# Routed expert layer on one core: slot numbers of all blocks fetched once ahead of the loop, gathers queued ahead of scatters, last expert's second weight half loaded later

## What is computed

```python
logits = (xf @ router_w + router_b)
top_vals, top_idx = lax.top_k(logits, TOP_K)      # 4 of 32 experts
gates = jax.nn.softmax(top_vals, axis=-1)
...
def expert_block(args):
    xblk, e = args
    h = xblk @ w1[e] + b1[e]
    g, u = jnp.split(h, 2, axis=-1)
    g = jnp.minimum(g, SWIGLU_LIMIT)
    u = jnp.clip(u, -SWIGLU_LIMIT, SWIGLU_LIMIT)
    act = g * jax.nn.sigmoid(SWIGLU_ALPHA * g) * (u + 1.0)
    return act @ w2[e] + b2[e]
...
y = jnp.zeros((N, D)).at[row_tok].add(yb * row_w[:, None])
```

## Time and profile before

| | |
|---|---|
| median of 3 runs | 2829.48 us (2829.42 to 2830.85) |
| profiled execution, its own time | 2824.4 us |
| its span, first to last instruction | 2822.6 us |
| mean granted TensorE clock | 0.948 |
| PE (matmul) busy | 2552.1 us, 90% of the span |
| DVE / ACT / POOL busy | 744.7 / 362.4 / 499.3 us |
| DMA bytes | 511.69 MB, of them 472.48 MB in SP's queue |

### The profile page before, as it was taken

One profiled execution on the slowest core, in us unless ns is written; L12 is line 12 of the kernel. 1 busy time (PEld: TensorE's weight loads), 2 busy tenths in 40 slices (PEclk: granted clock), 3 DMA queues, 4 the chain that ended last, 5 costly groups with the idle time before them and its releaser, 6 DMA issues.

```text
span 2822.6 us, 59253 instructions
## 1 busy us (share of the span) xinstructions
PE 2552.1 (90%) x22930; PEld 1090.6 (39%) x22931; DVE 744.7 (26%) x2075; ACT 362.4 (13%) x920; POOL 499.3 (18%) x639
## 2 busy tenths in 40 slices
PE   8999899999989769879998997997997999989984
PEld 4644556544435423223332332332332433323322
DVE  4441456411024412112221221221221222212212
ACT  2000455400003200000000000000000000000002
POOL 0000000000001212122221222221222222222221
PEclk9999899999999879889998998998998999999987
DMA  4110000400044495989689767668528357273464
GB/s 141 60 45 0 8 8 1 146 26 23 15 142 146 115 368 208 407 343 341 253 311 406 291 227 294 224 224 310 201 66 332 124 170 274 63 277 121 166 231 142
DMA packets 159463, 511.69 MB, mean 181 GB/s; under 512 B 37540, under 2 KB 73892, under 8 KB 125380
## 3 DMA queue, kind: packets, MB, share of 16 engines
q1 hardware_dynamic: 110576, 472.48, 43.1%
q0 software_dynamic: 29168, 38.39, 7.2%
q10 hardware_dynamic: 19668, 0.15, 0.4%
HBM read 479.16 MB, written 32.15 MB: 181 GB/s over the span
## 4 chain that ended last, share of the span: by engine, by line
PE 39%; DMA 23%; SPq 4%; issue 2%; DVE 1%; ACT 0%; ACTq 0%; POOL 0%; DVEq 0%; POOLq 0%
PE xbank L1487 21%; PE xbank L1510 13%; DMA big<-in_w 10%; DMA idxa<-slot_rows 9%; DMA loop_s<-xn_rows,idxg 4%; PE xbank L1443 4%; SPq L1034 2%; SPq L1039 1%; PE xbank L1497 1%; DMA acc_rows<-loop_s,idxs 0%; PE xbank L1504 0%; DVE big L1404 0%; PE xbank L1428 0%; DVE loop_s L1368 0%; ACT loop_s L1156 0%
## 5 line engine op out<-in xcount | busy, mean ns | idle before, releaser
L1487 PE MATMUL xbank<-big,loop_s 128*32 128x512 f32 x9280 | 1101.6, 612 | 134.0 <-DMA big<-in_w 109.9
L1487 PEld LDWEIGHTS xbank<-big,loop_s 128*32 128x32 f32 x9280 | 282.9, 111 | 788.2 <-issue 602.5
L1510 PE MATMUL xbank<-big,loop_s 128*32 128x256 f32 x9280 | 540.1, 386 | 0.0
L1368 DVE TENSOR_SCALAR loop_s<-xbank 128x256 f32<-128x256 f32 x145 | 61.6, 425 | 1301.3 <-PE xbank L1487 1301.3
L1510 PEld LDWEIGHTS xbank<-big,loop_s 128*32 128x32 f32 x9280 | 288.6, 112 | 247.7 <-issue 63.0
L1150 ACT ACTIVATE loop_s<-loop_s 128x256 f32<-128x256 f32 x145 | 60.5, 417 | 1658.7 <-DVE loop_s L1368 1635.4
L607 PE MATMUL pair<-big 128*128 128x512 f32 (+1 forms) x640 | 253.6, 551 | 0.2 <-DMA big<-in_w_in 0.2
L1086 POOL DMA_INDIRECT acc_rows<-loop_s,idxs x145 | 230.9, 1593 | 123.4 <-POOL idxs L1083 72.5
L1083 POOL TENSOR_TENSOR idxs<-idxa,tok 128x1 int32<-128x1 int32 x145 | 41.7, 288 | 941.9 <-ACT loop_s L1156 796.7
L1076 POOL DMA_INDIRECT loop_s<-xn_rows,idxg x147 | 145.8, 992 | 120.2 <-POOL idxg L1073 112.6
L607 PEld LDWEIGHTS pair<-big 128*128 128x128 f32 x640 | 119.3, 191 | 114.8 <-issue 110.8
(11 more groups left out here) (234 smaller groups left out, 1722.4 us busy)
## 6 DMA issues: line engine op xcount, KB each, us to landing
big<-in_w SPq DMA_DIRECT2D x396, 1024.0 KB, 12.9
big<-in_x SPq DMA_DIRECT2D x16, 512.0 KB, 5.0
big<-in_w_in SPq DMA_DIRECT2D x4, 2048.0 KB, 8.0
big<-in_w_in SPq DMA_DIRECT2D x16, 512.0 KB, 4.0
big<-in_w_o SPq DMA_DIRECT2D x1, 4096.0 KB, 26.9
acc_rows<-big SPq DMA_DIRECT2D x8, 512.0 KB
xn_rows<-big SPq DMA_DIRECT2D x8, 512.0 KB, 4.5
big<-acc_rows SPq DMA_DIRECT2D x8, 512.0 KB, 8.1
```

What stands on the lines that cost most here:

```text
L1368: dve.tensor_scalar(gl, up_bank[b][:, 0:FG], SWIGLU_LIMIT, None, ALU.min).then_inc(gate_min, 1)
L1487: ins = pe.matmul(up_bank[b][QB * c:QB * c + QB, :].rearrange("p (h k q) -> p h k q", h=2, q=QB), xT[b][:, QB * k:QB * k + QB], w1k[b][k]. ...
L1510: ins = pe.matmul(y_bank[b][QB * j:QB * j + QB, 0:DG], actT[b][:, QB * k:QB * k + QB], w2r[b][:, k, j * DG:(j + 1) * DG], start=False, sto ...
```

## The change

Ahead of the loop, POOL now issues two indirect DMAs that fetch the table rows of all blocks (one table row of 32 slots to a partition, blocks 0 to 127 and 40 to 167). DVE adds the group numbers and spreads them, PE transposes the result, and DVE copies it into `idx_all` and `gate_all`, a column for each block. `load_slots` and its waits are gone from ACT. POOL copies a column where it added two. POOL has four gathers ahead of the loop instead of three, and in the loop gather(2i + 4) and gather(2i + 5) stand ahead of scatter(2i) and scatter(2i + 1). On DVE, choose(n + 1) with its wait for `y_done` now stands ahead of swiglu(n) and turn_x(n + 2). The planner computes the row numbers as two columns over 128 partitions where it had one row of 168. SP waits for `raw_in` in place of `tab_out`, and for `idx_ready` besides, before it loads pieces 4 to 7 of the last expert's w1. The order of the other loads is what it was: the last expert's w2 (L1018) stands where it stood.

```diff
-            sp.wait_ge(tab_out, 16 * NT * TOPK)
+            sp.wait_ge(raw_in, 32)
             for n in range(2):
                 sp.wait_ge(xn_out[n], 16 * NT // 2)
             sp.wait_ge(list_ready, 1)
+            sp.wait_ge(idx_ready, 1)
             for k in range(4, KD):
                 load_last(k)
...
-            def gather(n, b, half, reused):
-
-                pool.wait_ge(idx_in[b], half * 16 + 16)
+            def gather(n, b, reused):
+
                 if reused:
                     pool.wait_ge(xT_ready, n - 1)
-                pool.tensor_tensor(idxg[b][:, :], idxa[:, bass.ds(n, 1), 0], group, ALU.add).then_inc(idxg_ready, 1)
+                pool.tensor_copy(idxg[b][:, :], idx_all[:, bass.ds(n, 1)]).then_inc(idxg_ready, 1)
...
-            gather(0, 0, 0, False)
-            gather(1, 1, 0, False)
-            gather(2, 0, 1, True)
+            pool.wait_ge(tab_out, 16 * NT * TOPK)
+            pool.wait_ge(rows_ready, 1)
+            for c in range(2):
+                pool.indirect_dma_start(out=raw[:, c].rearrange("p q v -> p (q v)"), out_offset=None, in_=raw_d,
+                                        in_offset=bass.IndirectOffsetOnAxis(ap=row_i[:, c:c + 1].bitcast(U32), axis=0)).then_inc(raw_in, 16)
             n_iters = block_iters(pool)
+            pool.wait_ge(idx_ready, 1)
+            gather(0, 0, False)
+            gather(1, 1, False)
+            gather(2, 0, True)
+            gather(3, 1, True)
             with pool.Fori(0, PAIRS) as i:
                 with pool.If(i < n_iters):
-                    gather(i * 2 + 3, 1, i + 1, True)
+                    gather(i * 2 + 4, 0, True)
                     scatter(i * 2, 0)
-                    gather(i * 2 + 4, 0, i + 2, True)
+                    gather(i * 2 + 5, 1, True)
                     scatter(i * 2 + 1, 1)
...
-            load_slots(4, 0, 2)
             with act.Fori(0, PAIRS) as i:
                 with act.If(i < n_iters):
                     for m in range(2):
-                        n = i * 2 + (m + 1)
-                        sigmoid(n)
+                        sigmoid(i * 2 + (m + 1))
                         weigh_y(i * 2 + m, m)
-                        load_slots(i * 2 + (m + 5), 1 - m, i + (2 + m))
...
+            dve.wait_ge(raw_in, 32)
+            dve.tensor_copy(tok_n, raw[:, :, :, 0])
+            for c in range(2):
+                dve.tensor_copy(spread[:, 2 + c], raw[:, c, :, 1].bitcast(F32).unsqueeze(1).to_broadcast([P, NG, QB]))
+            dve.drain()
+            for c in range(2):
+                ins = dve.tensor_tensor(spread[:, c], tok_n[:, c].unsqueeze(1).to_broadcast([P, NG, QB]),
+                                        iota_e[:, 0:NG].unsqueeze(2).to_broadcast([P, NG, QB]), ALU.add)
+            ins.then_inc(spread_ready, 1)
+            dve.wait_ge(spread_turned, 1)
+            rest = 2 * P - NPAD
+            dve.tensor_copy(idx_all[:, 0:P], bank[4][:, 0:P])
...
+            dve.drain()
+            dve.sem_inc(idx_ready, 1)
...
                     for m in range(2):
                         n = i * 2 + (m + 1)
+                        dve.wait_ge(y_done, n)
+                        choose(n + 1, m)
                         swiglu(n, 1 - m)
                         turn_x(n + 2, 1 - m, i + (m + 1))
-                        dve.wait_ge(y_done, n)
-                        choose(n + 1, m)
...
+            pe.wait_ge(spread_ready, 1)
+            for w in range(4):
+                ins = pe.transpose(bank[4][:, w * P:(w + 1) * P], spread[:, w].rearrange("p j q -> p (j q)"), ident)
+            ins.then_inc(spread_turned, 1)
```

More of the change, by code:

```diff
@@ L894, in expert_half @@
         step_e = l32[:, 704:800]
+        n_all, odd_last, turn_2, dummy_2, row_2 = (stage[:, 4 * D + 1024 + 4 * n:4 * D + 1026 + 4 * n] for n in range(5))
         l_cols = l32[:, 800:864]
-        row_f, dummy_f = lists[0:1, 1024:1024 + NPAD], lists[0:1, 1200:1200 + NPAD]
-        over_n = lists[0:1, 1400:1402]
         loop_s = sb("loop_s", [P, 11 * DG])
@@ L909, in expert_half @@
         iota_e, iota_32e, iota_se = fcs[:, 0:32], fcs[:, 32:64], fcs[:, 64:96]
-        upto, ones_f, follow = fcs[0:32, 96:128], fcs[0:32, 128:224], fcs[0:32, 224:256]
+        upto, ones_f, follow = fcs[0:32, 96:128], fcs[0:32, 128:256], fcs[0:32, 272:304]
+        odd_c, back_c, even_c = fcs[:, 264:265], fcs[:, 265:267], fcs[:, 267:269]
         part_c = fcs[:, 256:257]
         key_mul, key_add, time_add, load_mul, load_add, next_c, expert_c = (fcs[0:32, 257 + n:258 + n] for n in range(7))
-        turn_c = loop_s[0:32, 8 * DG:8 * DG + 4 * NPAD]
-        odd_n, not_odd_n, back_n, even_n = (turn_c[:, n * NPAD:(n + 1) * NPAD] for n in range(4))
+        turn_c = loop_s[0:32, 8 * DG:8 * DG + 3 * NPAD]
+        odd_n, not_odd_n, back_n = (turn_c[:, n * NPAD:(n + 1) * NPAD] for n in range(3))
+        raw = part[2][:, 0:2 * 2 * QB].bitcast(I32).rearrange("p (c q v) -> p c q v", c=2, v=2)
+        tok_n = part[3][:, 0:2 * QB].rearrange("p (c q) -> p c q", c=2)
+        spread = loop_s[:, 4 * DG:4 * DG + 4 * P].rearrange("p (w j q) -> p w j q", w=4, j=NG)
         tri, ones_b, one_b = bcs[:, 0:P], bcs[:, P:2 * P], bcs[:, 256:257]
@@ L1082, in scatter @@
                 pool.wait_ge(rows_added, n * 16 + 32)
-                pool.tensor_tensor(idxs[b][:, :], idxa[:, bass.ds(n, 1), 0], group, ALU.add).then_inc(idxs_ready, 1)
+                pool.tensor_copy(idxs[b][:, :], idx_all[:, bass.ds(n, 1)]).then_inc(idxs_ready, 1)
                 pool.wait_ge(idxs_ready, n + 1)
@@ L1137, in _ @@
                     store_xn(t - 1)
-            def load_slots(n, b, half):
-                if not (isinstance(half, int) and half == 0):
-                    act.wait_ge(idx_in[b], half * 16)
-                row = act.value_load(listi[0:1, 1, bass.ds(n, 1)], min_val=0, max_val=TABROWS - QB)
-                act.dma_start(idxa[:, bass.ds(n, 1), :].rearrange("p o v -> p (o v)"),
-                              tab_d[bass.ds(row, QB), :].unsqueeze(0).to_broadcast([NG, QB, 2])).then_inc(idx_in[b], 16)
             def sigmoid(n):
@@ L1320, in _ @@
             dve.tensor_tensor(late_c, n_c, time_add, ALU.add)
-            dve.tensor_scalar(iters_i[0:1, :], listi[0:1, 0, 0:1], 1, None, ALU.arith_shift_right)
+            dve.tensor_scalar(turn_2, back_c, odd_last[:, 0:1], None, ALU.add)
+            dve.tensor_scalar(iters_i[0:1, :], listi[0:1, 0:1], 1, None, ALU.arith_shift_right)
             dve.drain()
```

77 lines of the change are left out of this document (40 added, 37 removed).

## The result

The changed kernel takes **2757.4 us** (median of 4 runs, 2755.0 to 2758.3) against 2829.45 us (2827.7 to 2830.9) for the kernel before, timed beside it: ratio 0.9744, 95% interval 0.9728 to 0.9761, or 72 us less. The forecast was 2790 us with a range from 2780 to 2809, so the direction was right and the size was not: 72 us came off where 39.5 were promised. The profiled execution took 2757.98 us with a span of 2756.0; before it was 2824.4 with 2822.6. Between the two profiled executions lie 66.6 us of span.

What follows compares the result with a forecast made beforehand. Weight bytes were taken to bound stretches of successive loads, late `sel` those with lone loads. -38.5 (lone loads) - 1 (index traffic) + 0 = -39.5 us from 2829.5 gave 2790 us, range 2780 to 2809.

Steps and rivals of the forecast that it cites:

- two kinds of stretches: Expert loop: where weight loads follow each other, bytes set the time; where a load comes alone, PE waits only for `sel`.
- the pace of 10.65 us: Expert loop: time of one block that waits for nothing, from four blocks in 42.61 us.
- the lone loads: Five stretches with single weight loads, 88 blocks: 975.69 us against 937.2 at pace, so 38.5 us to be removed.
- the waits for `sel`: PE at the bias matmul: 43.1 us in 30 waits, to vanish or stay below 3 us.
- The start: Before the first block: one-time fetch, spreading and first gather cost 0, at the outside 5 us; PE begins at 1008 (1014.3).
- The scatters: POOL's shared queue: rival that scatters fall behind gathers and hold up `weigh_y`, slower, to 2934 us; chance 0.04.
- The end that went by ACT's fetch: At the start: late case where the new fetch takes 12.1 us, `idx_ready` at 1006.8 and PE beginning at 1014.3.
- ACT's queue took 0.4% of the DMA engines' time: Full stretches: removing index fetches there, about 42 at 0.076 us each, saves at most 3.2 us, taken as 1.
- the bytes set the time: Stretches of successive weight loads: DMA shares 1.00 and 0.97, so removing a PE wait only makes PE wait for weights.
- the early gathers as a second cover: POOL's gathers issued some 19 us before use, against 8.96 at worst: covers the same `sel` waits, adds nothing to the sum.
- weights take the place: Lone weight loads: rival that half of 38.5 us returns as waits for weights, about 2809 us; chance 0.15.
- The median: Whole kernel: the runs' median stays 5.1 us above the profiled execution, turning 2785 into 2790 us.

Runs made afterwards that it cites:

- experiment 9: The changed kernel with SP also waiting for `xT_ready` before loading w1's last pieces, some 7 us later: 2759.4 us, ratio 0.9765.
- experiment 1: The kernel before with only choose(n + 1) and its wait for `y_done` moved ahead of swiglu(n) and turn_x(n + 2): 2794.9 us, ratio 0.988.
- experiment 3: The changed kernel plus 149 unread ACT fetches, 32 rows read four times as 128 pieces of 8 bytes, on four engines: 2832.0 us, ratio 1.0018.
- 14: The kernel before with each real index fetch issued as four of 32 rows, spread over all engines: 2790.5 us, ratio 0.9865.
- 7: The kernel before with both new orders (choose ahead, gathers ahead of scatters), its index fetches kept and read: 2800.4 us, ratio 0.9892.
- experiment 2: The changed kernel with both old orders back (choose behind turn_x, gathers behind scatters), only the one-time table fetch left: 2757.9 us, ratio 0.974.
- experiment 6: The changed kernel plus 149 unread four-engine fetches, each row read four times, source moving on 256 bytes per fetch: 2781.9 us, ratio 0.9835.
- 15: The kernel before with choose moved ahead and each index fetch issued as four on all engines: 2771.1 us, ratio 0.9796.
- experiment 13: The changed kernel plus 149 unread fetches of the same 32 rows, each read four times, on 16 engines: 2771.9 us, ratio 0.98.
- experiment 12: The changed kernel plus 149 unread fetches of 128 different rows, on four engines: 2770.0 us, ratio 0.9797.
- 5: The changed kernel plus 149 unread fetches of 128 different rows, 128 pieces of 8 bytes, on 16 engines: 2769.2 us, ratio 0.9786.
- 10: The changed kernel plus 149 unread fetches of 128 different rows, viewed as four times 32 but lying on 16 engines: 2764.7 us, ratio 0.9785.
- 11: The changed kernel plus 149 unread fetches of 128 different rows on 16 engines, source starting at neighbouring rows: 2762.5 us, ratio 0.9776.
- 4: The changed kernel plus 149 unread fetches, each one row of 256 bytes in one piece: 2757.3 us, ratio 0.9739.

## Why the prediction missed

**Right, by its own steps.** The bound and the split into two kinds of stretches; the pace of 10.65 us; the lone loads (-38.5 forecast, -38.1 measured); the waits for `sel` gone; the waits for weights within 10 us of 109.9 (109.0). The start: fetch 6 us forecast, 5.6 measured; spreading 4, measured 3.0; PE began at 1002.9, 5 us ahead of the 1008 named, and 4.0 of it is the earlier landing of the table. The start has slack (experiment 9); the 2.3 us that the prediction let an issue take to reach the engines were 1.0 us wherever the queue was empty, which adds to it. The scatters did not fall behind either: POOL's waits for them stood at 147 us (145 before), and PE waited for none. The end that went by ACT's fetch of the earlier trace rows, 12.1 us, did not come. The rule of the Trainium skill that was weighed there (DMA: Bandwidth & Descriptors, "Issuing engine by pattern": SP's and ACT's DMAs are generally faster) pointed to that end, and the trace did not follow it here; the two fetches differ in their pieces too, 256 bytes against 8.

**Wrong: a term that was mis-sized.** The step was "ACT's queue took 0.4% of the DMA engines' time ... at most 3.2 us; I take 1". It priced the fetches by the time of their own packets. The stretches where the bytes set the time gave 19.2 + 4.0 = 23.2 us, seven times that bound. `choose` alone gives 3.8 of it (experiment 1); from there to the change, with the fetches gone, the windows give 15.4, blocks 3 to 18 4.9 and the lone loads 9.4 us. Experiment 3 shows a price by itself: 75 us for 149 fetches that no one reads, at a share of 0.4%. The step averaged a fetch over 16 engines, while it lies on four and a weight piece waits for the slowest one. Priced so, the bound would have been 4 x 3.2 = 12.8 us (an estimate from its own numbers), nearer but still too small, for the four engines trail by 2.7 us at the end of a load while a fetch's packets take 0.3 us on an engine (32 of 9 ns) and some four fetches fall into a load. With real fetches it is 39 us for their form alone (14) and 43 for all that `choose` does not give (7). The same step failed once more in the prediction: the earlier trace rows were read as "the bytes set the time", at 375 and 400 GB/s in two windows. The shares there, 0.97 and 1.00, stand below the 1.03 that the kernel after reached; the two rates were a hint that not all engines were busy all the time, and in the last microsecond of the window to 2175 only four of them are at work (the row of 2174 in experiment 3).

**Right in sum, wrong in part.** The 38.5 us of the lone loads were to be taken by `choose` alone, with the early gathers as a second cover. Experiment 1 shows that it takes 28.7 of them, because with the fetches in place PE then runs into waits for weights; experiment 2 shows that the table alone takes 36.7 with the old orders. The forecast named the right sum and the wrong part, so that the lone loads came out within 0.4 us is in part luck. The rival "weights take the place" was held to be unlikely at 0.15; without the fetches it did not come, and with them it took a quarter of what was recovered (9.8 of 38.5). Its price has a slip: 2829.5 - 19 is 2810.5 and not 2809, which changes nothing in the outcome.

**The median.** The forecast carried the 5.1 us by which the profiled execution lay below the median over to the kernel after. There this gap was absent, which is worth 5.7 us of the 32.6 by which the forecast was too high. The other 26.9 are the full stretches (23.2 less the 1 taken), the start (6.2 - 0.8 = 5.4) and the lone loads (-0.4), together 27.2, where the spans are 27.1 away from the forecast.

**What stays open.** Why reading the same rows stops an engine, and only at some fetches, why the rows of experiment 6 cost 50 us less, and why half of the fetches make the four engines trail nearly as much as all. The kernels with the longest windows are those in which four engines trail by 2.7 us or more (385.9 to 397.3 us), but experiments 6 and 15 have 384.5 and 381.5 us at a lag of 0.2 us, so the lag is not the whole price. And the real fetches cost 43 us by experiment 7 where the unread ones cost 75: their rows lie elsewhere in the table and they are issued at other moments, and no run keeps these two apart.

## What to carry to other kernels

Price a small DMA beside a saturated stream by what the stream loses, not by its own share of the engines: 149 fetches of 1 KB at 0.4% cost up to 75 us here, and the test is cheap, since the same fetches can be issued with nobody reading them. Write a replicated small load so that its slowest dimension spreads it over all engines and so that engines do not read the same rows together, or fetch it once in long pieces. And where windows with a nearly full DMA share show different rates, look at the end of the load, where it shows whether all engines finish together, before taking the bytes as the bound.

## What the runs showed of the hardware

A 1 MiB load over 16 engines has landed when the last of them is done. With 149 fetches of 128 pieces of 8 bytes on four engines that read the same rows, those four end a load 2.7 us (before) or 4.1 us (experiment 3) behind the others, and 0.1 to 0.2 us without the fetches or with them on 16 engines. For blocks 89 to 93 the rate is then 390 GB/s at a DMA share of 0.99 to 1.00, and 396 to 408 at 1.00 to 1.03 without the fetches or with another form.

Where a fetch reads rows more than once, engines stopped for a moment at one of some four fetches of a window: a share of 0.31 for 2 us on all 16 (experiment 13), of 0.74 for 2.5 us on four (experiment 3). In the same place the share was 1.01 where the rows differ (experiment 12).

Reading 1 KB as 128 pieces, 149 times, costs 5 to 14 us in the medians when no more than one of the two properties is there (experiments 5 and 10 to 13; 9 to 16 us by the ratios), nothing when 256 bytes come in one piece, 24 us on four engines that read the same near rows, new ones each time (6), and 75 us at 4096-byte multiples with rows that come again from block to block (3). A fetch issued in a full stretch lands after 13 to 14 us on four engines and 6 to 7 on 16. Splitting one DMA into four, each on all engines, made the kernel 39 us faster.

The kernel before spread from 2817 to 2841 us over all its runs, the kernels without fetches or with one piece for each (the change and experiments 2 and 4) from 2755.0 to 2762.8. The first are 49 runs in six sets and the second 12 in two, so that the fetches make the time spread is likely and not shown.
